# A two-block transformer kernel: weighing the modulation rows on VectorE instead of TensorE, and splitting the load of constants

## The reference

```python
mod_l = jax.nn.silu(c) @ w_ada[l] + b_ada[l]
sh_l, sc_l, gt_l = jnp.split(mod_l[:, None, :], 3, axis=-1)
mod_c = jax.nn.silu(c_ctx) @ w_ada[l] + b_ada[l]
h_l = _rmsnorm(x, g_pre[l]) * (1.0 + sc_l) + sh_l
br_a = ((a_b * _short_conv(a_c * a_x, conv_w_l)) * jax.nn.silu(a_z)) @ w_br_conv_l
```

## Time and profile before

| | |
|---|---|
| median of three runs | 4289.35 us |
| the profiled execution, its own time | 4284.67 us |
| its span in the trace | 4282.8 us |
| PE busy in the span | 3980.4 us, 93% |
| DVE busy | 1640.3 us, 38% |
| ACT busy | 955.3 us, 22% |
| POOL busy | 1791.6 us, 42% |
| stage conv0 (8 turns) | 1274.7 to 1602.5 us of the span |
| PE's first instruction | 23.03 us |

### The profile page before, as it was taken

How to read it: one execution, slowest core, us unless ns; L and a number is a source line. 1 busy time by engine, 2 the same in 40 slices (tenths; PEclk the granted TensorE clock), 3 DMA queues, 4 the chain that set the end, 5 groups by cost and what they waited for, 6 DMA issues and landing times. The chain is left out here.

```text
span 4282.8 us, 52308 instructions
## 1 busy us (share of the span) xinstructions
PE 3980.4 (93%) x19915; PEld 3093.7 (72%) x19915; DVE 1640.3 (38%) x2520; ACT 955.3 (22%) x1697; POOL 1791.6 (42%) x770
## 2 busy tenths in 40 slices
PE   6999999999989999899999998998899999999999
PEld 5777788888878887576678777776685445877744
DVE  1444426656631123344425555445215554122100
ACT  2333312222210001333312222011214443011000
POOL 1333352332325544344454343687442212877600
PEclk7899999999999998899999999998888998999999
DMA  6111221111236543222232211334421101333322
GB/s 187 44 42 51 60 63 45 47 46 41 51 81 120 103 93 103 59 59 52 72 68 60 50 50 47 98 89 123 124 60 41 50 15 37 93 101 83 89 78 73
DMA packets 512281, 305.18 MB, mean 71 GB/s; under 512 B 37769, under 2 KB 492818, under 8 KB 511210
## 3 DMA queue, kind: packets, MB, share of 16 engines
q1 hardware_dynamic: 500010, 282.43, 27.0%
q10 hardware_dynamic: 12096, 20.33, 1.3%
HBM read 276.42 MB, written 26.27 MB: 71 GB/s over the span
## 5 line engine op out<-in xcount | busy, mean ns | idle before, releaser
L852 POOL TENSOR_TENSOR whi<-ring,con 128x1024 fp32r<-128x1024 f32 (+2 forms) x383 | 893.2, 2332 | 2216.9 <-DMA ring<-in_w_in 1736.7
L541 PE MATMUL ps<-xT_parts,whi 128*128 128x512 f32 (+2 forms) x2600 | 996.7, 383 | 63.1 <-DVE hT_parts L2083 35.4
L541 PE MATMUL ps<-hT_parts,whi 128*128 128x512 f32 (+1 forms) x2856 | 1046.1, 366 | 0.0
L541 PE MATMUL ps<-xT_parts,ring_parts 128*128 128x512 f32 (+2 forms) x2600 | 945.1, 363 | 0.0
L854 POOL TENSOR_TENSOR ring_parts<-ring,whi 128x1024 fp32r<-128x1024 f32 (+2 forms) x383 | 900.2, 2350 | 30.0
L1535 ACT ACTIVATE arena<-ps 128x512 f32<-128x512 f32 (+7 forms) x583 | 311.4, 544 | 1769.0 <-PE ps L541 1016.5
L541 PE MATMUL ps<-arena_parts,whi 128*128 128x512 f32 (+1 forms) x2112 | 640.6, 381 | 67.1 <-DVE arena_parts L2077 59.3
L541 PE MATMUL ps<-arena 128*128 128x128 f32 (+9 forms) x3292 | 645.3, 340 | 28.0 <-DVE arena L2045 22.4
L541 PEld LDWEIGHTS ps<-xT_parts,whi 128*128 128x128 f32 (+1 forms) x2600 | 494.4, 190 | 169.0 <-issue 66.8
L541 PEld LDWEIGHTS ps<-hT_parts,whi 128*128 128x128 f32 x2856 | 542.8, 190 | 90.5 <-issue 7.0
L541 PEld LDWEIGHTS ps<-arena 128*128 128x128 f32 (+3 forms) x3292 | 437.5, 193 | 181.4 <-issue 123.1
(11 more groups left out here) (147 smaller groups left out, 3467.1 us busy)
## 6 DMA issues: line engine op xcount, KB each, us to landing
ring<-in_w_in SPq DMA_DIRECT2D x504, 256.0 KB, 3.9
arena<-in_w_ada SPq DMA_DIRECT2D x64, 256.0 KB, 4.9
ring<-in_w_up SPq DMA_DIRECT2D x64, 256.0 KB, 4.0
ring<-in_w_down SPq DMA_DIRECT2D x64, 256.0 KB, 3.7
ring<-in_w_out SPq DMA_DIRECT2D x48, 256.0 KB, 3.7
gates_kept<-stage ACTq DMA_DIRECT2D x24, 384.0 KB, 3.8
arena<-gates_kept SPq DMA_DIRECT2D x24, 384.0 KB, 3.7
ring<-in_w_ada SPq DMA_DIRECT2D x32, 256.0 KB, 3.9
```

Source lines behind the costliest of these rows:

```text
L541: return nc.tensor.matmul(o, l, r, start=first, stop=last)
L852: v.tensor_tensor(hi, raw, ones[:, 0:m].unsqueeze(1).to_broadcast([P, kt, m]), ALU.mult).then_inc(w_rounded, 1)
```

## The change

The block of `w_ada` that a turn needs is now loaded as 4 slots of 256 rows x 512 columns. DVE weighs it: for each of the 8 slices of 128 rows and each of the two vectors one instruction of 128 x 512 that multiplies by the vector's element on that partition and adds to `mod_sum` (2 x 512 columns). Four slices are weighed ahead of the turn's z product, four behind it. PE sums `mod_sum` over partitions behind tile 3 with 8 matmuls of one column against ones. `mod_summed` releases all four slots at once. The constants come in two transfers: 640 columns first, and 5376 columns behind the first four tiles of ada0, which DVE waits for only ahead of the first rotary product (`tables_in`).

```diff
--- before.py
+++ after.py
@@ -315,7 +315,9 @@
 
         rounded = take(KT * ALL)
 
-        mod_ring = take(4, KT, P, at=used[0] - KT * ALL)
+        mod_ring = take(4, 2, 512, at=used[0] - KT * ALL)
+        mod_sum = take(2, 512)
+        used[0] += KT * ALL - 5 * 1024
         gin = arena[:, base:base + 4 * ALL].rearrange("p (s n) -> p s n", s=4)
 
         more = base + 15424
@@ -450,10 +452,12 @@
         part_hi, part_lo = sem("part_hi"), sem("part_lo")
         h_ready, h_scaled, h_hi, h_lo = sem("h_ready"), sem("h_scaled"), sem("h_hi"), sem("h_lo")
         mod_landed, mod_used = [sem(f"mod_landed{s}") for s in range(4)], sem("mod_used")
+        mod_summed = sem("mod_summed")
         x_kept, x_back, x_new = [sem(f"x_kept{h}") for h in range(2)], sem("x_back"), sem("x_new")
         pair_free = [sem(f"pair_free{s}") for s in range(2)]
 
         phase, inputs_in, out_done = sem("phase"), sem("inputs_in"), sem("out_done")
+        tables_in = sem("tables_in")
         act_own, dve_own = sem("act_own"), sem("dve_own")
         x_turned, par_turned = sem("x_turned"), sem("par_turned")
         sq_ready, sq_used, ms_done, rs_ready = sem("sq_ready"), sem("sq_used"), sem("ms_done"), sem("rs_ready")
@@ -635,7 +639,8 @@
                 n, w = src.shape
                 sp.dma_start(dst[r:r + n, c0:c0 + w], src).then_inc(inputs_in, 16)
 
-            sp.dma_start(con[:], a["con"]).then_inc(inputs_in, 16)
+            first_con = C_AT["cos"][0]
+            sp.dma_start(con[:, 0:first_con], a["con"][:, 0:first_con]).then_inc(inputs_in, 16)
             sp.dma_start(y_in[:, 0:LT, :], a["x"][0].rearrange("(t p) f -> p t f", p=P)).then_inc(inputs_in, 16)
             sp.dma_start(y_in[:, LT:NT, :], a["ctx"][0].rearrange("(t p) f -> p t f", p=P)).then_inc(inputs_in, 16)
 
@@ -687,6 +692,7 @@
 
                     for s in range(4):
                         load(a["w_ada"][0][:, s * P:(s + 1) * P])
+                    sp.dma_start(con[:, first_con:], a["con"][:, first_con:]).then_inc(tables_in, 16)
                     sp.wait_ge(phase, 3 * phases_to("load"))
                     keep_x(ALL)
                     with sp.Fori(0, 3) as i, tiles.loop(i, 3, 4):
@@ -706,7 +712,7 @@
                         if mods_of:
 
                             if not isinstance(i, int) or i > 0:
-                                sp.wait_ge(mod_used, i * 4 + (s - 3))
+                                sp.wait_ge(mod_summed, i)
                             else:
                                 sp.wait_ge(phase, 3 * phases_to("branch2_0"))
                             load_mod(s, mods_of(s))
@@ -756,9 +762,9 @@
                 if l == 0:
 
                     for i in range(2):
-                        conv(i, lambda s: a["w_ada"][0][:, (16 + 4 * i + s) * P:(17 + 4 * i + s) * P])
+                        conv(i, lambda s: a["w_ada"][0][256 * s:256 * s + 256, (16 + 4 * i) * P:(20 + 4 * i) * P])
                     with sp.Fori(0, 6) as i, tiles.loop(i, 6, 4):
-                        conv(i + 2, lambda s: a["w_ada"][1][:, ds(i * 512 + s * P, P)])
+                        conv(i + 2, lambda s: a["w_ada"][1][256 * s:256 * s + 256, ds(i * 512, 512)])
                 else:
                     with sp.Fori(0, KT) as i, tiles.loop(i, KT, 4):
                         conv(i)
@@ -1055,18 +1061,17 @@
                 else:
                     mean_square(ALL)
 
-                def conv(i, cond):
+                def conv(i, with_mods):
                     for s in range(4):
                         turned_tile(hP, n)
-                        if cond is None:
-                            continue
-
-                        pe.wait_ge(mod_landed[s], i * 32 + 32)
-                        if s == 0:
+                        if s == 3 and with_mods:
+                            pe.wait_ge(mod_summed, i + 1)
                             pe.wait_ge(mod_read, i)
-                        for k in range(KT):
-                            last = mm(bank(6)[:, 2 * s:2 * s + 2], mod_ring[:, s, k], cond[:, :, k], k == 0, k == KT - 1)
-                        last.then_inc(mod_used, 1)
+                            for m in range(4):
+                                for c in range(2):
+                                    last = mm(bank(6)[:, 2 * m + c:2 * m + c + 1], mod_sum[:, c, m * P:(m + 1) * P],
+                                              ones[:, 0:1], True, True)
+                            last.then_inc(mod_used, 1)
 
                 def norm_mm(c, m, free=None):
 
@@ -1296,14 +1301,8 @@
                 branch(n)
                 if phase_end(f"branch2_{l}"):
                     return
-                if l == 0:
-                    with pe.Fori(0, 2) as i, tiles.loop(i, 2, 4), uses.loop(i, 2, 4), splits.loop(i, 2, 4):
-                        conv(i, conds[0])
-                    with pe.Fori(0, 6) as i, tiles.loop(i, 6, 4), uses.loop(i, 6, 4), splits.loop(i, 6, 4):
-                        conv(i + 2, conds[1])
-                else:
-                    with pe.Fori(0, KT) as i, tiles.loop(i, KT, 4), uses.loop(i, KT, 4), splits.loop(i, KT, 4):
-                        conv(i, None)
+                with pe.Fori(0, KT) as i, tiles.loop(i, KT, 4), uses.loop(i, KT, 4), splits.loop(i, KT, 4):
+                    conv(i, l == 0)
                 if phase_end(f"conv{l}"):
                     return
                 branch(n)
@@ -2167,6 +2166,7 @@
                     dve.wait_ge(qn_ready, c + 1)
                     v.tensor_tensor(dst[:, 0:LAT], rope_t, rope_s, ALU.add).then_inc(q_ready, 1)
 
+                dve.wait_ge(tables_in, 16)
                 nb = NORMED * l
                 qg, kg = par[l][:, R_QG:R_QG + 1], par[l][:, R_KG:R_KG + 1]
                 for c in range(2):
@@ -2369,11 +2369,30 @@
                     own(v.memset(conv_u[:, e:e + 1], 0.0))
                 stretches = [(0, 0, LAT)] + ([(LAT + 2, LAT, CTX)] if n == ALL else [])
                 ns = len(stretches)
-                with dve.Fori(0, KT) as i, tiles.loop(i, KT, 4), uses.loop(i, KT, 4), own.loop(i, KT, 4 * ns):
+                def weigh_mods(i, ks):
+
+                    for k in ks:
+                        if k % 2 == 0:
+                            dve.wait_ge(mod_landed[k // 2], i * 32 + 32)
+                        own.settle()
+                        for c in range(2):
+                            m_, c_ = mod_ring[:, k // 2, k % 2], conds[1][:, c, k:k + 1]
+                            if k == 0:
+                                own(v.tensor_scalar(mod_sum[:, c], m_, c_, None, ALU.mult))
+                            else:
+                                own(stt(mod_sum[:, c], m_, c_, mod_sum[:, c], ALU.mult, ALU.add))
+
+                with dve.Fori(0, KT) as i, tiles.loop(i, KT, 4), uses.loop(i, KT, 4), own.loop(i, KT, 4 * ns + 16 * (l == 0)):
+                    if l == 0:
+                        weigh_mods(i, range(4))
                     p = product()
                     dve.wait_ge(z_tanh, i + KT * l + 1)
                     last_read()
                     stt(tmp[:, 0:n], tha[:, 0:n], 1.0, pair(p, n), ALU.add, ALU.mult).then_inc(pair_free[p], 1)
+                    if l == 0:
+                        weigh_mods(i, range(4, KT))
+                        own.settle()
+                        v.memset(stat[:, 3, 6:7], 0.0).then_inc(mod_summed, 1)
                     skip()
                     last_read()
                     skip()
@@ -2403,7 +2422,7 @@
                     skip()
                     if l == 0:
 
-                        dve.wait_ge(mod_used, i * 4 + 4)
+                        dve.wait_ge(mod_used, i + 1)
                         v.tensor_copy(mods[:, ds(i * 4 + 16, 4)], bank(6, 8).rearrange("p (a b) -> p a b", a=4)).then_inc(mod_read, 1)
                 if l == 0:
                     dve.wait_ge(mod_read, KT)
```

## The result

| | before | changed |
|---|---|---|
| time, us, median (lowest to highest, runs) | 4289.59 (4285.13 to 4291.8, 4) | 4256.68 (4252.52 to 4264.64, 4) |
| ratio, 95% interval | 1 | 0.9927 [0.9914, 0.9939] |
| profiled execution, us | 4284.67 | 4264.64 |
| span of stage conv0, us | 327.9 | 304.3 |

The kernel is faster by 32.9 us in the medians, 36 were summed and the predicted 4250 is 6.7 us short. The profiled execution of the changed kernel is the longest of its four, that of before is shorter than all four in the table, so the two traces differ by 20.0 us only. Of these 23.6 are gained in the stage, 0.7 are lost up to its start (1275.2 us for 1274.5) and 2.9 behind it (2683.3 us for 2680.4).

What follows compares the result with a forecast made beforehand. PE was taken to bound stage conv0, and DMA bytes ahead of the tables the start. Matmuls 44.2, less 6 (settled turns) and 9 (first two turns), plus 7 (constants) gave 36 us off 4284.67; it said 4250, range 4235 to 4275.

Runs made afterwards that it cites:

- e4: Changed kernel with the weighing's running sums in PSUM, only the last slice writing mod_sum; 4242.33 us, ratio 0.9883 to the kernel before.
- e10: Changed kernel with running sums in PSUM and each w_ada block issued behind the next tile (blocks 2, 3 behind tile 3); 4240.04 us, 0.988 of before.
- e7: Changed kernel with running sums in PSUM and blocks 0 and 1 released after the first four slices; 4249.07 us, ratio 0.99 to the kernel before.

## What to carry to other kernels

When work goes from PE to DVE, count the other engine's instructions that fall beside it, and not DVE's busy time; an accumulation whose running sum lies in PSUM costs 0.75 us a step here whatever POOL does, one in SBUF 0.75 us for a step that meets no split and 2.8 for one that does. Look at what the new semaphore holds back in the queue that waits for it: here a wait for the whole sum kept three tiles of weights back, and a tile moved ahead of it was worth 10 us of stage. And judge a head start by several traces: 6.9 us of it were worth 1.9 us by one pair of traces and 6.7 by another, as the granted clock fell out.

## What was not expected of the hardware

- A tensor_scalar of 128 x 512 takes 0.49 us from SBUF to SBUF and 0.74 with its result in PSUM (all 16 in e4). The slower one lost nothing within a split of POOL; the fast one, 1.57 us in the mean of after, did.
- After 5.9 us of idling in one place PE's granted clock is 0.92 over that turn of 44.2 us, which costs it 3.0 us more. In e10, where PE never waits in the stage but for the pause ahead of it, the clock is 0.99.
- PE's head start was partly given back at once in the profiled run: 3.0 us in the stretch behind it at 0.86, 2.1 in ada0 (52.0 for 49.9). In e7 none of it was.
- A block of the same bytes in rows four times as long costs SP the same two issues of 0.6 us.
